# The low part of the fourth weight behind a LayerNorm: GpSimd ahead of its centring, or VectorE between two normalised tiles

## The reference, cut to what matters

```
for i in range(DEPTH):                       # DEPTH = 2
    mods = (silu(c) @ ada_w[i] + ada_b[i]).reshape(bsz, 9, D_MODEL)
    h = x * (1 + mods[:, 1]) + mods[:, 0]
    y = (silu(a) * b) @ w_out                # a, b = split(h @ w_in)
    x = layer_norm(ALPHA * x + 0.5 * mods[:, 2] * y, ln_g[i, 0], ln_b[i, 0])
    h = x * (1 + mods[:, 4]) + mods[:, 3]
    y = attention(h) if i == 0 else hgrn2(h)
    x = layer_norm(ALPHA * x + mods[:, 5] * y, ln_g[i, 1], ln_b[i, 1])
    ...                                      # the second FFN in the same way
```

## Time and profile before

| | us |
|---|---|
| median of 3 executions (2138.68 to 2141.26) | 2140.7 |
| the profiled execution, its own time | 2141.63 |
| its span | 2139.9 |
| TensorE matmul busy | 2097.4 |
| VectorE busy | 1199.3 |
| ScalarE busy | 784.7 |
| GpSimd busy | 246.0 |

### The profile page before, as it was taken

One profiled execution on the slowest core, in us unless ns is written; L12 is line 12 of the kernel. 1 busy time (PEld: TensorE's weight loads), 2 busy tenths in 40 slices (PEclk: granted clock), 3 DMA queues, 4 the chain that ended last, 5 costly groups with the idle time before them and its releaser, 6 DMA issues.

```text
span 2139.9 us, 30931 instructions
## 1 busy us (share of the span) xinstructions
PE 2097.4 (98%) x10775; PEld 1720.5 (80%) x10775; DVE 1199.3 (56%) x1878; ACT 784.7 (37%) x1142; POOL 246.0 (11%) x238
## 2 busy tenths in 40 slices
PE   7999999999999999999999999999999999999997
PEld 5788888878888888888888888877878788888886
DVE  6766665655557666654535533467676555333344
ACT  4321222455434222222532222376666545322222
POOL 0000000432113000001300000151121131000002
PEclk9999999999999999999999999999999999999999
DMA  9766752332325657643335632332222123323322
GB/s 319 216 184 196 219 174 72 88 109 80 106 70 186 188 176 226 195 125 101 89 98 164 179 98 76 101 102 77 70 77 69 40 70 99 91 85 113 95 73 84
DMA packets 405669, 266.34 MB, mean 124 GB/s; under 512 B 9416, under 2 KB 366184, under 8 KB 405608
## 3 DMA queue, kind: packets, MB, share of 16 engines
q1 hardware_dynamic: 405608, 265.57, 41.5%
HBM read 263.37 MB, written 2.19 MB: 124 GB/s over the span
## 4 chain that ended last, share of the span: by engine, by line
PE 92%; ACT 3%; DVE 3%; issue 1%; POOL 1%; DMA 0%; SPq 0%; ACTq 0%; POOLq 0%; DVEq 0%
PE ps L1483 26%; PE ps L1485 26%; PE ps L1484 26%; PE ps L1498 1%; PE ps L1499 1%; PE ps L1523 1%; PE ps L1761 1%; PE ps L1504 1%; PE ps L1682 1%; PE ps L1708 1%; PE ps L1529 1%; PE ps L1693 1%; DVE w_lo L837 1%; PE ps L1779 1%; PE ps L1515 1%
## 5 line engine op out<-in xcount | busy, mean ns | idle before, releaser
L837 DVE TENSOR_TENSOR w_lo<-raw,w_hi 128x1024 fp32r<-128x1024 f32 (+2 forms) x384 | 429.1, 1119 | 699.4 <-ACT w_hi L601 699.2
L601 ACT ACTIVATE w_hi<-raw 128x1024 fp32r<-128x1024 f32 (+2 forms) x384 | 371.6, 969 | 1104.9 <-PE ps L1485 1067.2
L1483 PE MATMUL ps<-h_hi,w_hi 128*128 128x512 f32 x1744 | 686.8, 394 | 3.6 <-DVE g L846 2.2
L1485 PE MATMUL ps<-h_hi,w_lo 128*128 128x512 f32 x1744 | 679.4, 390 | 0.0
L1484 PE MATMUL ps<-h_lo,w_hi 128*128 128x512 f32 x1744 | 678.9, 389 | 0.0
L1483 PEld LDWEIGHTS ps<-h_hi,w_hi 128*128 128x128 f32 x1744 | 327.4, 188 | 79.0 <-issue 8.3
L1485 PEld LDWEIGHTS ps<-h_hi,w_lo 128*128 128x128 f32 x1744 | 327.4, 188 | 68.9
L1484 PEld LDWEIGHTS ps<-h_lo,w_hi 128*128 128x128 f32 x1744 | 327.6, 188 | 65.9
L1483 PE MATMUL ps<-g_hi,w_hi 128*128 128x512 f32 x704 | 276.0, 392 | 0.0
L1485 PE MATMUL ps<-g_hi,w_lo 128*128 128x512 f32 x704 | 274.1, 389 | 0.0
L1484 PE MATMUL ps<-g_lo,w_hi 128*128 128x512 f32 x704 | 274.0, 389 | 0.0
(11 more groups left out here) (252 smaller groups left out, 1943.6 us busy)
## 6 DMA issues: line engine op xcount, KB each, us to landing
raw<-in_ffn_w_in_dram SPq DMA_DIRECT2D x176, 512.0 KB, 3.7
ada_raw<-in_ada_w_dram SPq DMA_DIRECT2D x128, 512.0 KB, 4.3
raw<-in_ffn_w_out_dram SPq DMA_DIRECT2D x64, 384.0 KB, 3.4
raw<-in_ffn_w_out_dram SPq DMA_DIRECT2D x64, 320.0 KB, 3.1
raw<-in_hgrn_w_in_dram SPq DMA_DIRECT2D x40, 512.0 KB, 3.7
raw<-in_na_w_qkv_dram SPq DMA_DIRECT2D x24, 512.0 KB, 3.7
boot<-in_ada_w_dram SPq DMA_DIRECT2D x8, 512.0 KB, 6.8
boot<-in_ada_w_dram SPq DMA_DIRECT2D x16, 256.0 KB, 6.1
```

Source lines behind the costliest of these rows:

```text
L601: nc.scalar.activation(w_hi[s][:, 0:ph.kt, :], raw[s][:, 0:ph.kt, :], ACT.Copy).then_inc(S.w_hi_done, 1)
L837: nc.vector.tensor_tensor(w_lo[s][:, 0:ph.kt, :], raw[s][:, 0:ph.kt, :], w_hi[s][:, 0:ph.kt, :].bitcast(F32), ALU.subtract).then_inc(S.w_l ...
L1483: nc.tensor.matmul(ps[:, bank, :], w_hi[s][:, k, :], a, start=start and k == 0, stop=False)
L1485: ins = nc.tensor.matmul(ps[:, bank, :], w_lo[s][:, k, :], a, start=False, stop=stop and k == ph.kt - 1)
```

## The change

VectorE's `convert(nxt, 0, 3)` is gone from `after`. GpSimd gets `fourth_low`, the same subtraction with the same operands, and calls it in front of its `centre`. It waits for the low parts of weights 0 to 2 (to keep the order of the count) and for ScalarE's high part of the fourth, and raises `w_lo_done` itself. At the end of VectorE's `after` a wait keeps its later low parts behind it.

```diff
--- before.py
+++ after.py
@@ -1212,8 +1212,6 @@
                 for k in range(1, DVE_CENTRED):
                     centre(k)
                     normalise(k)
-                if nxt is not None and nxt.body > 3:
-                    convert(nxt, 0, 3)
                 for k in range(DVE_CENTRED, KT):
                     normalise(k)
                     low_parts(n + 1, k - DVE_CENTRED)
@@ -1221,6 +1219,8 @@
                     low_parts(n + 1, k)
                 low_parts(n + 1, KT - 2)
                 low_parts(n + 1, KT - 1)
+                if nxt is not None and nxt.body > 3:
+                    dve.wait_ge(S.w_lo_done, nxt.u0 + 4)
 
             def finished():
                 dve.wait_ge(S.rstd_done, NLN)
@@ -1324,6 +1324,12 @@
                     nc.gpsimd.tensor_scalar(x[:, k, :], x[:, k, :], AG[:, n, k:k + 1], AB[:, n, k:k + 1],
                                             ALU.mult, ALU.add).then_inc(S.x_ready, 1)
 
+            def fourth_low(nxt):
+                pool.wait_ge(S.w_lo_done, nxt.u0 + 3)
+                pool.wait_ge(S.w_hi_done, nxt.u0 + 4)
+                nc.gpsimd.tensor_tensor(w_lo[3][:, 0:nxt.kt, :], raw[3][:, 0:nxt.kt, :], w_hi[3][:, 0:nxt.kt, :].bitcast(F32),
+                                        ALU.subtract).then_inc(S.w_lo_done, 1)
+
             def centre(ph):
 
                 n = ph.ln
@@ -1431,7 +1437,7 @@
                                             ALU.mult).then_inc(S.qg_done, 1)
 
             first = True
-            for ph in phases:
+            for ph, nxt in zip(phases, phases[1:] + [None]):
                 if ph.kind == "na":
                     pool.wait_ge(S.unit_done, ph.u0)
                     make_mask()
@@ -1462,6 +1468,8 @@
                     for j in range(tiles - 1):
                         add_up(ph, ph.iters - 1, j, tiles)
                     if ph.ln < NLN - 1:
+                        if nxt is not None and nxt.body > 3:
+                            fourth_low(nxt)
                         centre(ph)
                         next_residual(ph.ln)
                     else:
```

## The result

The changed kernel takes **2147.07 us** (median of 19), the kernel before, run beside it, 2141.67 us (median of 19, 2138.68 to 2144.06): ratio **1.0025 [1.0019, 1.0031]**, 5.4 us slower. The forecast was 2141.6 us, 0.9 more than the 2140.7 it started from, so it was wrong; its rival B had 2146.7. Of the changed kernel's executions 18 lie between 2144.88 and 2148.95 us, and one, disturbed, took 3520.78 us; the ratio is without it. The profiled execution of the changed kernel took 2146.5 us (span 2144.6).

A forecast was written before the change was run, and what follows sets the result against it. TensorE was taken to bound the kernel (92% of the chain's span). Terms 2 x 0.7 - 0.5 + 0 = +0.9 us on the 2140.7 us median gave 2141.6 us, range 2139.0 to 2146.7.

The forecast's parts named there:

- rival B: Behind the second spread, the gap keeps the clock low another stretch: +1.7 us at three norms, 2146.7 us; chance 0.15.
- the 0.7 us taken for the second and third norm: Cost per norm of TensorE's 1.0 us gap, partly covered by half-clock work, with a pipeline refill; bounds 0.5 and 1.2.
- The size of the gap: TensorE empty ahead of the second spread at the third norm, waiting for the late reciprocal: 1.0 us.
- GpSimd's instruction: The added GpSimd subtraction over 128x1024 takes 2.42 us, with bounds of 1.30 and 3.4 us.
- rival D: Writing the rounded type makes GpSimd's subtraction twice as slow, 4.8 us: +7.4 us, 2148.1 us; chance 0.08.
- The hold: In the statistics, VectorE's L1200 waits for GpSimd's instruction to end: 1.9 us instead of 0.17, ending 1.73 us late.
- C: Rival: VectorE's small instructions in the statistics aren't held, only the gain stays: -1.5 us, 2139.2 us; chance 0.17.
- Removal at norms 2 and 3: Taking VectorE's conversion away is worth 0 there, since h_hi(4) already has 0.8 us in hand at the third norm.
- The fourth norm's gain: Without the conversion, normalise(0) to the low pass takes 13.41 us as at the first norm, not 14.88: 1.47 us gained.
- the fourth norm: Net term there: normalise(0) comes 0.9 us later, less the 1.47 us gained, gives -0.5 us.
- The fifth: Fifth norm's net term: statistics come slower, so VectorE is 0.6 us late, before TensorE is ready: 0.
- The load of slot 3: Slot 3 of raw comes free sooner, so SP's next load goes out some 7 us sooner: worth 0.

The follow-up runs named there:

- e8: The changed kernel, but GpSimd's subtraction waits for VectorE's L1200 (var_done), so it starts just behind it; 2140.79 us, ratio 0.9998 against the kernel before.
- e5: The kernel before with the same GpSimd subtraction added, while VectorE's own low part stays in its old place; 2147.89 us, ratio 1.0032.
- e6: The kernel before with VectorE's conversion moved behind its last low part at the fourth norm alone, nothing on GpSimd; 2143.85 us, ratio 1.0013.
- e2: The changed kernel with GpSimd's subtraction cut into two instructions of 128x512 at the same place; 2141.73 us, ratio 1.0002 against the kernel before.
- e7: The kernel before with VectorE's conversion and half of another moved between L1197 and L1200, nothing on GpSimd; 2148.94 us, ratio 1.0032.

## Why the prediction was wrong

**The step that failed** is one sentence: "If the clock rises at the same moment, an empty 1.0 us replaces half-clock work, which needs only 0.5 us when redone at 2.4 GHz", and with it the 0.7 us taken for the second and third norm. The clock didn't rise at the same moment. The two norms cost 2.12 and 2.71 us, 1.4 and 2.0 above the term; rival B's price for another stretch of 3.4 us was 1.7. Of the 0.7, 0.2 was for a refill of the pipeline that no row shows. So B is what happened, at two norms of the three it named. That its 2146.7 lies 0.4 from the median of 2147.07 is in part luck: with two norms B's own sum is 0.9 + 2 x 1.7 = +4.3 us, and the rest came mainly from the 1.40 us gap at the fourth norm, which cost its whole length. At the fourth, the stretch began at 1407.4, 5.1 us behind L869, with most of the gap before it, and lasted 3.4 us.

**The size of the gap.** I expected 1.0 us; it was 1.40 at norms 3 and 4, 0.61 at the second. The second spread was where I put it: 5.39 us behind L869, expected 1031.6 - 1026.06 = 5.5. What differed is the work ahead: at the third norm the half-clock stretch began at 1031.9, behind the first spread and the one keep_busy, so these ran at 2.4 GHz (1.14 and 0.47 us) and TensorE was done sooner. The stretch then fell on the gap and on the keep_busy matmuls behind it.

**Right, with its number.** GpSimd's instruction: 2.42 us forecast, here four of them (ns min/median/max, first and last start):

```profile
L1330 POOL TENSOR_TENSOR w_lo<-raw,w_hi x4: 2339/2346/2347, 649.2 to 1759.0; 128x1024 fp32r<-128x1024 f32 x4
```

It writes the rounded type at no extra cost, so rival D falls. The hold: 1.90 us forecast for L1200, 1.81, 1.82, 1.82 and 1.64 measured, so C falls. The Trainium skill (GPSIMD Engine Reference, section "Key points") has GpSimd contend with VectorE instructions in a 2-port mode or with two SBUF inputs. The SCALAR_TENSOR_TENSOR with one input in PSUM, free at 0.16 us, is of neither kind, which agrees. The tensor_scalar (held, 1.82 us) and the reciprocal (free, 0.18 us) have one SBUF input each; they agree if the first ran in a 2-port mode and the second didn't, which no run here shows. L1194, with two SBUF inputs, never began inside GpSimd's instruction. Removal at norms 2 and 3: 0 forecast; in e8, without a hold, they take 22.88 and 22.90 us, as before. At the fifth too 0 was forecast; there the clock differs between the traces, and they can't tell. The fourth norm's gain: 1.47 us forecast, 1.36 measured in the first pass of the changed kernel (1.02 against e5, 1.31 in e6, and 1.61 in e8 where nothing else moved).

**Of the other terms**, the fourth norm was to give -0.5 and gave +0.12: normalise(0) came 1.33 us late, not 0.9, since the clock gave no discount on the gap. The fifth was to give 0 and gave +0.19: its statistics were not slower this time (L1200 3.2 us behind L869, before 4.6), the hold was full, and a stretch of 6.8 us stands in both kernels. The load of slot 3 did go out sooner, 651.67 instead of 659.30 at the second norm, and changed nothing. Sum of the terms: 0.9 forecast, 5.1 measured.

**What the profile would have allowed.** The rows of the fifth norm already showed that a stretch can last 6.9 us, and that TensorE's work then comes 1.6 us later (24.55 for 22.9 us). The hold took away array work just where the clock was low. I gave this 0.15 and called the filled 2.4 of 3.4 us evidence against; nothing in the trace said that this is enough. Over all eleven traces, a gap ahead of the second spread at norms 2 and 3 (0.37 to 1.48 us) came with 6.8 us or more at half clock in six cases of six; without one it was so in one case of sixteen (e6, norm 2). At the fourth norm a gap of 1.4 or 1.5 us left 3.4 us in three cases of three. Why the fourth is spared is open: its stretches began later, but what sets the start wasn't tried.

## What to carry to other kernels

When work moves to GpSimd, list VectorE's small tensor_scalar instructions that fall beside it: each waits for the end of the whole GpSimd instruction, 1.82 us here instead of 0.17. If one stands on the way to TensorE, start GpSimd behind it (one wait brought back all 5.4 us) or cut the instruction in two. And price a gap of TensorE beside a stretch at half clock at its length or more, not at half of it: 0.6 and 1.4 us of gap cost 2.1 and 2.7 us at two norms, and 1.4 us cost about 1.5 at the fourth (+0.12 with the 1.36 gained there).

## What the runs showed of the hardware

- Stretches at 1.2 GHz lasted 3.4, 6.8 or 10.2 us at the first five norms of all eleven traces. Where one begins moves from execution to execution: at the first norm, where e2, e6 and e7 have the same instructions as the kernel before, these three have a stretch of 3.4 us (19.75, 19.28 and 19.39 us), the kernel before and the changed one none (18.34 and 18.35). So one trace of a place isn't enough to say that its clock is covered, and a difference of 1.4 us at one norm between two traces can be this alone.
- The hold goes in both directions, and in e6 a waiting GpSimd instruction wasn't let in between VectorE's: a tensor_scalar on 128x512 began at 1420.84, took 3.83 us (before 1.73) and ended only behind the third of three back-to-back subtractions, 1420.29 to 1424.19. VectorE's L1200 did get in between two of GpSimd's in e2: held from 1030.26 to 1030.99, while the second half is on record from 1030.93.
- GpSimd's time for two inputs in SBUF goes with the size beyond a small start: 0.737, 1.298 and 2.346 us for 256, 512 and 1024 elements. The rounded output costs nothing more: the halves of 512 in e2 take 1.26 and 1.27 us.
